# Moving the softmax steps of a windowed attention to other weight jobs of a two-layer hybrid block

## The reference

```python
h = rms_norm(x, g_mix)
b_a, c_a, x_a, u_p, q, k, v, ga, gp, gt = split(h @ w_in)
y_a = (b_a * depthwise_conv3(c_a * x_a)) @ w_a_out
y_p = multiscale_pool(u_p) per group @ w_pool[group] * pool_scale
y_t = windowed_gqa(q, k, v, rel_bias, sink) @ w_attn_out
x = x + (sigmoid(ga)*y_a + sigmoid(gp)*y_p + sigmoid(gt)*y_t) @ w_o
h2 = rms_norm(x, g_ffn);  x = x + (silu(gate) * up) @ w_down
```

## Time and profile before

| what | value |
|---|---|
| time, median of 3 runs | 1366.69 us (1366.68 to 1366.88) |
| the profiled execution | 1366.68 us, of which the span of its instructions is 1364.8 us |
| PE busy | 1325.1 us (97%) |
| DVE busy | 1038.1 us (76%) |
| ACT busy | 737.3 us (54%) |
| DMA | 262 MB, 192 GB/s over the span |
| granted TensorE clock | 0.996 of full speed |

### The profile page before, as it was taken

The page is one execution under the profiler, slowest core; times in us unless marked ns, Lnnn a source line. Parts: engine busy times, 40 slices in busy tenths (PEclk is TensorE's granted clock), DMA queues, the critical chain, the costliest instruction groups (busy, mean ns, idle before and its releaser), DMA issues.

```text
span 1364.8 us, 22597 instructions
## 1 busy us (share of the span) xinstructions
PE 1325.1 (97%) x8928; PEld 1192.3 (87%) x8928; DVE 1038.1 (76%) x1786; ACT 737.3 (54%) x1154; POOL 42.7 (3%) x80
## 2 busy tenths in 40 slices
PE   7999999999999999999999999999989998999998
PEld 6989999998888889999999988888868876888886
DVE  4387668786778784776687776787888888688888
ACT  5354765544445454546744354454467776655553
POOL 1000000000000000000000000000010000000000
PEclk9999999999999999999999999999999999999999
DMA  9965534554778665444345655777625513345551
GB/s 270 217 247 192 186 125 158 207 212 166 256 270 291 247 218 199 155 155 155 130 149 178 243 197 196 273 284 261 236 92 171 226 53 124 112 182 193 203 191 63
DMA packets 42147, 262.00 MB, mean 192 GB/s; under 512 B 5229, under 2 KB 5613, under 8 KB 14782
## 3 DMA queue, kind: packets, MB, share of 16 engines
q1 hardware_dynamic: 32688, 227.28, 47.1%
q0 software_dynamic: 9264, 33.24, 7.6%
q10 hardware_dynamic: 94, 0.07, 0.0%
HBM read 258.99 MB, written 1.58 MB: 191 GB/s over the span
## 4 chain that ended last, share of the span: by engine, by line
PE 83%; DVE 9%; DMA 4%; ACT 3%; issue 1%; SPq 0%; DVEq 0%; ACTq 0%
PE psum L697 21%; PE psum L717 15%; PE psum L814 12%; PE psum L703 10%; PE psum L723 8%; PE psum L762 4%; DMA ring<-stream 3%; DVE split L1772 3%; PE psum L769 2%; PE psum L788 2%; PE psum L849 1%; PE psum L872 1%; PE psum L862 1%; PE psum L981 1%; DVE arena L1765 1%
## 5 line engine op out<-in xcount | busy, mean ns | idle before, releaser
L1772 DVE TENSOR_TENSOR split<-ring,split 128x1024 fp32r<-128x1024 f32 x408 | 482.4, 1220 | 115.9 <-ACT split L1288 114.7
L1288 ACT CAST split<-ring 128x1024 fp32r<-128x1024 f32 x407 | 408.0, 1050 | 184.2 <-PE psum L703 84.1
L697 PE MATMUL psum<-h,split 128*128 128x256 f32 x2176 | 276.6, 285 | 2.1 <-ACT split L1288 2.1
L697 PEld LDWEIGHTS psum<-h,split 128*128 128x128 f32 x2176 | 266.5, 192 | 11.2 <-issue 10.1
L717 PE MATMUL psum<-h,split 128*128 128x512 f32 x960 | 229.0, 390 | 0.7 <-ACT split L1288 0.7
L717 PEld LDWEIGHTS psum<-h,split 128*128 128x128 f32 x960 | 177.7, 188 | 36.4 <-DVE arena L2567 1.1
L814 PE MATMUL psum<-split,feed 128*128 128x512 f32 x792 | 186.0, 391 | 1.3 <-DVE feed L1772 0.7
L814 PEld LDWEIGHTS psum<-split,feed 128*128 128x128 f32 x792 | 146.6, 188 | 31.6 <-DVE split L1772 1.5
L703 PE MATMUL psum<-h,split 128*128 128x256 f32 x1088 | 141.7, 283 | 0.0
L703 PEld LDWEIGHTS psum<-h,split 128*128 128x128 f32 x1088 | 135.5, 192 | 0.0
L723 PEld LDWEIGHTS psum<-h,split 128*128 128x128 f32 x960 | 123.3, 191 | 4.8
(11 more groups left out here) (328 smaller groups left out, 1398.8 us busy)
## 6 DMA issues: line engine op xcount, KB each, us to landing
ring<-stream SPq DMA_DIRECT2D x213, 1024.0 KB, 4.9
arena<-ada POOLq DMA_DIRECT2D x48, 512.0 KB, 5.3
arena<-bias_by_distance POOLq DMA_DIRECT2D x8, 384.0 KB, 30.6
gain<-norm_rows POOLq DMA_DIRECT2D x4, 512.0 KB, 6.8
x<-x_in SPq DMA_DIRECT2D x2, 512.0 KB, 4.6
ring<-stream SPq DMA_DIRECT2D x2, 512.0 KB, 7.4
gain<-mod_rows POOLq DMA_DIRECT2D x2, 512.0 KB, 5.0
out<-x SPq DMA_DIRECT2D x4, 256.0 KB, 2.0
```

The source lines that it names most:

```text
L697: pe.matmul(to[m], w[0][:, at + k, cols[m]], rhs[:, part, at + k, :], start=m == parts[0] and k + part == 0, stop=False)
L1288: act.copy(split_of(x)[:, 0, n], ring[:, AT[x] % RING, n]).then_inc(wh_ready, 1)
L1772: return dve.tensor_tensor(out_, value, high.bitcast(F32), ALU.subtract)
```

## The change

The change gives the 19 steps of each layer to other jobs. It adds and removes no instruction of a step. Without steps stay, in both versions, the u jobs and wa3.

```diff
-ATT_EARLY = [JOB["c", 0] + i for i in (2, 3, 5, 6, 8, 9, 11)] + [JOB["ga", 0] + i for i in range(7)]
-ATT_LAYER = ([{k: i for i, k in enumerate(ATT_EARLY + [JOB["gp", j] for j in range(4)] + [JOB["wp", 3]])}]
-             + [{k: i for i, k in enumerate([JOB["c", 0]] + ATT_EARLY + [JOB["gp", j] for j in range(4)])}] * (L - 1))
+ATT_EARLY = [JOB["c", 0] + 1 + 2 * i for i in range(6)] + [JOB["ga", 0] + i for i in (0, 2, 3, 5, 6)]
+ATT_LAYER = ([{k: i for i, k in enumerate(ATT_EARLY + [JOB["gp", 0] + i for i in range(8)])}]
+             + [{k: i for i, k in enumerate([JOB["c", 0]] + ATT_EARLY + [JOB["gp", 0] + i for i in range(7)])}] * (L - 1))
```

## The result

| | before | after |
|---|---|---|
| median | 1366.68 us (1364.92 to 1366.88, 4 runs) | 1380.53 us (1376.18 to 1383.45, 4 runs) |
| profiled execution | 1366.68 us, span 1364.8 us | 1376.32 us, span 1374.5 us |
| granted clock | 0.996 | 0.991 |

The ratio is 1.0097 with a 95% interval of 1.0081 to 1.0114: 13.3 us slower (11.1 to 15.6). The forecast was 1378.4 us, + 11.75. The two profiled executions themselves lie 9.6 us apart, less than the medians; where the rest of that pair went is told at the end.

A forecast was written before the change was run, and what follows sets the result against it. PE, busy 97% of the span, was taken as the bound, so only its waits could change. From 1366.68: + 7.1 + 4.9 − 1.25 − 0.30 + 1.3 = + 11.75, so 1378.4 us; range 1370 to 1382.

The forecast's parts named there:

- The backlog and the round: gp jobs: ACT and DVE rounds of 7.54 us against PE's mean 7.60, first `exps` 8.86 us after gp0, never catching up.
- The waits of the wp jobs: Steps moved to gp and wp jobs: new PE waits summing to 7.1 us in layer 0, 4.9 in layer 1.
- The early part: c, x, b, ga and wa jobs: moved steps cost nothing; the wait of `scores(1)` in layer 0 goes, minus 1.25 us.
- The 0.30 us of layer 1: Layer 1: the old PE wait before `turn(15)` goes, minus 0.30 us.
- The clock: gt0 of layer 0: granted clock falls to 0.5 for about 3 us after the 2.5 us wait, plus 1.3 us, bounds 0 to 2.6.
- The dearer table switch: Rival, gp jobs: 1.38 us drain on each exposed table load, plus 8.3 us, 1386.7; chance of above 1382 was 0.04.
- the start: Layer 0, step 0 moved to x0: `scores(1)` no longer waits, minus 1.25 us, bounds 0 and 1.25.

The follow-up runs named there:

- the kernel with filled waits: Changed kernel with 83 matmuls added behind wp0 and wp2 of layer 0, wp0 and wp1 of layer 1, where PE would wait: 1378.29 us, 1.0081 of before.
- the late part alone: Only gp and wp steps as after the change, the others at c and b jobs and four ga and wa jobs: 1380.06 us, 1.0095 of before.
- the second measurement: The changed kernel run again, unchanged, beside other experiments: 1377.85 us, 1.0084 of before.
- the kernel with the shorter u3: Changed kernel with two of four running additions of u3's pool left out on DVE, ahead of gp0: 1374.96 us, 1.0062 of before.
- the first profile of the early part: Only c, x, b, ga and wa steps as after the change, gp and wp jobs as before; first of two runs: 1364.36 us, 0.9977 of before.

## Why the prediction was right, point by point

- *The backlog and the round.* Right to 0.1 us for each `exps`. Shown by two experiments: a round without table loads takes most of the loss away; DVE work ahead of gp0 cut by 1.5 us moves the whole chain by 1.5 us.
- *The waits of the wp jobs.* Forecast 0.4, 3.3, 0.9, 2.5 in layer 0; seen 0.46, 3.17, 0.78 and, for the last, slow matmuls in place of a wait. Layer 1: forecast 3.6 and 1.3; seen 3.32 and again slow matmuls. In the kernel with filled waits, where the clock is out of play, the sums are 6.6 and 4.8 us for 6.7 and 4.9 forecast.
- *The early part.* Its cost of nothing agrees with the runs, and the wait of `scores(1)` is gone in every profile with step 0 at x0. Its gain of 1.25 us was taken as fixed, and that is not shown: the wait was read from one execution in which a chunk was late, and it is missing in the late part alone, with the old placement and the chunk in time. The gain lies between 0 and 1.25 us, the bounds that the prediction gave, and is below what these measurements tell from no change, save in one that did not repeat.
- *The 0.30 us of layer 1.* Gone from `turn(15)` in gp2, as that step no longer stands there.
- *The clock* was the term put in the wrong place. I added 1.3 us for a fall at gt0 of layer 0. There was none: the fall came behind the first wait in both layers, lasted about 7 us and not 3, and the wait behind it took it in, wholly or but for 1.5 us in both layers together. The two profiles of the changed kernel lie 0.5 and 1.1 us and then 0.0 and 0.1 us over the kernel with the clock at 1.00. So the term is between 0 and 1.5 us and differs by execution; the 1.3 us that I added lie in that span, but for a fall that did not happen, while the real ones I had costed at nothing. That this term fits is luck. Its size was of the right order for a fall of 3 us: 1.5 us in the third block (below) and 1.6 at gt0 without table loads.
- *The dearer table switch.* The rounds stay at 7.54 us in the dense gp jobs, and shrink by 1.4 without the loads, little more than the 1.28 us of the exposed one. The second figure of the Trainium skill's page "ScalarE: Activation LUTs" (section "What ACT_TABLE_LOAD costs"), 1.38 us of drain on top of each load, would make it 2.66; it is not seen here.

Of the total, + 11.75 forecast and + 13.3 (11.1 to 15.6) or, in the second measurement, + 11.5 (8.1 to 15.0) measured, nothing is left that the scatter does not cover. The 12.0 us of waits, the core of the sum, are shown one by one (11.4 us with the clock out of play, and 0.46 before gp3). The two small terms that are not shown, − 1.25 for the start and + 1.3 for the clock, have opposite signs, so the total would be as close without both; this is no merit of the forecast.

## What to carry to other kernels

An engine in program order with a round as long as the bound engine's pace never loses its delay; a schedule that gives it a row of such rounds and then short jobs presents the delay all at once. Count the round from one profile, start to start, and lay it beside the pace of the jobs that it is to be spread over. And a wait that the profile names can be where the delay shows and not where it is made: here, taking the named copy out of the way moved 6.5 us of waits to other lines and made the kernel no faster.

## What the runs showed of the hardware

After waits of PE of 2.17, 3.17, 3.32 and 5.08 us in different kernels the granted clock was at 0.50 for some microseconds; after 1.21 and 1.80 us in layer 1 of the kernel with the shorter u3 it stayed at 1.00. Between these the length of the wait did not decide. The wait of the earlier trace rows in the third block is 1.83 to 1.98 us long in eleven of the thirteen profiles; behind it the clock fell in six, the kernel before among them, and stayed up in five, the changed kernel among them. Timeline and window of PE in the changed kernel there:

```profile
1039.50 1.09 PE L1006 MATMUL psum<-cst,arena 128*128 128x128 f32 x8 [1.85 <-DVE arena L2260]
1040.34 4.08 PE L697 MATMUL psum<-h,split 128*128 128x256 f32 x32
```
```profile
1039.00:1042.00 3.00, 2.50 (x22) 2.51 (x23) 3.00 (x7) 2.03 (x5) 0.00 (x0) 1.00 1.00 388
```

From these transposes to the low part of the job behind them PE needs 4.76 us here (1039.50 to 1044.26), and 6.30 in the kernel before (1028.84 to 1035.14). So a fall cost the kernel before 1.5 us that the changed kernel was spared in its profile. That is why the profiled executions are only 9.6 us apart: at gt0 of layer 1 the changed kernel is 10.6 us behind (751.73 for 741.11). Up to there it also waited less for early chunks in this pair, 0.3 us for 2.1.

What a fall cost depends on what stands behind it: 0 to 1.1 us where another wait followed, 1.5, 1.6 and 2.4 us where none did.

The early chunks are another source of scatter. In the first profile of the early part PE waited 1.99 us for a chunk, and then did its 32 matmuls in 5.4 us in place of 3.8. Timeline and window of PE there:

```profile
73.28 5.55 PE L697 MATMUL psum<-h,split 128*128 128x256 f32 x32 [1.99 <-ACT split L1288]
```
```profile
73.50:76.50 3.00, 3.00 (x16) 3.00 (x16) 2.96 (x7) 1.86 (x2) 0.00 (x0) 0.52 0.89 371
```

In the second profile of the same kernel all such waits are missing, and the stretch from the transposes of kd to wp0 in layer 0 is 190.3 us (50.66 to 240.94) in place of 195.9 (50.30 to 246.15). Of these 5.6 us three waits for chunks are 3.6 and the slow matmuls 1.5. Here too the length did not decide: in the second profile of the changed kernel PE waited 1.96 us for a chunk at the same place and kept its clock:

```profile
72.42 4.06 PE L697 MATMUL psum<-h,split 128*128 128x256 f32 x32 [1.96 <-ACT split L1288]
```
